# Weight casts and subtractions placed ahead of roots, reciprocals and the use of a finished unit, in a two-block model kernel on one Trainium2 core

## What is computed

```python
def rms_norm(x, g):
    xf = x.astype(jnp.float32)
    y = xf * lax.rsqrt(jnp.mean(xf * xf, axis=-1, keepdims=True) + RMS_EPS)
    return (y * g.astype(jnp.float32)).astype(x.dtype)
...
def conv_ffn(h, w_up, ffn_dw_w, ffn_dw_b, w_down):
    val, gate = jnp.split(h @ w_up, 2, axis=-1)
    gate = causal_dwconv(gate, ffn_dw_w, ffn_dw_b)
    return (jax.nn.silu(gate) * val) @ w_down
...
    h = x
    for l in range(DEPTH):
        u = rms_norm(h, norm_mix_g[l])
        h = h + mixer_sublayer(u, cos, sin, w_in[l], b_gate[l], ret_gn_g[l], w_ret_out[l],
                               conv_dw_w[l], conv_dw_b[l], conv_ln_g[l], conv_ln_b[l],
                               w_conv_out[l], b_conv_out[l], w_mix_out[l])
        mem_n = rms_norm(mem, norm_mem_g[l])
        h = h + memory_cross_attention(rms_norm(h, norm_xattn_g[l]), mem_n,
                                       w_xq[l], w_xkv[l], w_xo[l])
        h = h + conv_ffn(rms_norm(h, norm_ffn_g[l]), w_up[l], ffn_dw_w[l], ffn_dw_b[l], w_down[l])
    return rms_norm(h, norm_final_g)
```

## Time and profile before

| what | us |
|---|---|
| median of 3 runs | 2090.15 |
| lowest, highest | 2089.9, 2092.16 |
| the profiled execution, whole | 2091.13 |
| its span, first to last instruction | 2089.3 |
| TensorE busy in it | 2068.3 |
| VectorE busy | 1659.0 |
| ScalarE busy | 1055.8 |
| GpSimd busy | 257.6 |

### The profile page before, as it was taken

The page is one execution under the profiler, slowest core; times in us unless marked ns, Lnnn a source line. Parts: engine busy times, 40 slices in busy tenths (PEclk is TensorE's granted clock), DMA queues, the critical chain, the costliest instruction groups (busy, mean ns, idle before and its releaser), DMA issues.

```text
span 2089.3 us, 38625 instructions
## 1 busy us (share of the span) xinstructions
PE 2068.3 (99%) x16378; PEld 2015.3 (96%) x16378; DVE 1659.0 (79%) x2449; ACT 1055.8 (51%) x1282; POOL 257.6 (12%) x176
## 2 busy tenths in 40 slices
PE   9999999999999999999999999999999999999998
PEld 9999999999999999989999999999988999989998
DVE  8888797787779788798986768767698996758764
ACT  6786354356755434355545445444346445444442
POOL 0212055000006500001201001100000300000100
PEclk9999999999999999999999999999999999999999
DMA  6663455554235455544555435546544555534543
GB/s 262 193 199 125 182 185 184 170 212 150 101 142 182 157 187 202 181 158 162 199 178 174 177 141 182 176 159 212 182 164 150 192 182 182 182 139 167 182 163 118
DMA packets 58300, 361.95 MB, mean 173 GB/s; under 512 B 6736, under 2 KB 9360, under 8 KB 21136
## 3 DMA queue, kind: packets, MB, share of 16 engines
q1 hardware_dynamic: 58128, 359.48, 49.0%
HBM read 358.37 MB, written 1.08 MB: 172 GB/s over the span
## 4 chain that ended last, share of the span: by engine, by line
PE 95%; DVE 2%; ACT 1%; issue 1%; DMA 0%; POOL 0%; SPq 0%; DVEq 0%; ACTq 0%
PE acc L644 79%; PE acc L643 7%; PE acc L759 1%; PE acc L760 1%; PE acc L761 1%; PE acc L964 1%; PE pA L1013 1%; DVE w_lo L1196 0%; DMA raw<-in_wide 0%; PE pC L807 0%; PE pB L1037 0%; PE pD L1124 0%; PE pA L1099 0%; PE pB L1099 0%; PE pB L1124 0%
## 5 line engine op out<-in xcount | busy, mean ns | idle before, releaser
L644 PE MATMUL acc<-in_hi,w_hi 128*128 128x256 f32 x4656 | 1304.9, 285 | 9.8 <-issue 9.4
L644 PE MATMUL acc<-in_hi,w_lo 128*128 128x256 f32 x4656 | 1292.9, 283 | 0.1
L644 PE MATMUL acc<-in_lo,w_hi 128*128 128x256 f32 x4656 | 1230.2, 283 | 0.0
L644 PEld LDWEIGHTS acc<-in_hi,w_hi 128*128 128x128 f32 x4656 | 892.0, 192 | 16.2 <-issue 12.3
L644 PEld LDWEIGHTS acc<-in_hi,w_lo 128*128 128x128 f32 x4656 | 892.1, 192 | 0.6 <-DVE w_lo L1527 0.3
L644 PEld LDWEIGHTS acc<-in_lo,w_hi 128*128 128x128 f32 x4656 | 855.1, 192 | 1.2 <-issue 1.0
L1196 DVE TENSOR_TENSOR w_lo<-raw,w_hi 128x2048 fp32r<-128x2048 f32 (+1 forms) x341 | 737.3, 2164 | 112.7 <-ACT w_hi L2059 111.7
L2059 ACT CAST w_hi<-raw 128x2048 fp32r<-128x2048 f32 (+1 forms) x341 | 614.2, 1804 | 238.5 <-PE acc L644 227.6
L2659 POOL TENSOR_TENSOR in_lo<-arena,in_hi 128x256 fp32r<-128x256 f32 (+1 forms) x112 | 127.2, 1136 | 1212.4 <-ACT in_hi L2519 514.5
L1840 DVE SCALAR_TENSOR_TENSOR arena<-arena,cols 128x256 f32<-128x256 f32 x480 | 200.4, 487 | 0.0
L2669 POOL TENSOR_TENSOR arena<-arena 128x256 f32<-128x256 f32 x44 | 96.3, 2189 | 385.1 <-ACT arena L2341 385.1
(11 more groups left out here) (293 smaller groups left out, 1653.3 us busy)
## 6 DMA issues: line engine op xcount, KB each, us to landing
raw<-in_wide SPq DMA_DIRECT2D x285, 1024.0 KB, 4.8
raw<-in_narrow SPq DMA_DIRECT2D x64, 704.0 KB, 4.1
arena<-cs_rows SPq DMA_DIRECT2D x16, 256.0 KB, 5.0
arena<-in_mem SPq DMA_DIRECT2D x3, 1024.0 KB, 6.9
x<-in_x SPq DMA_DIRECT2D x4, 256.0 KB, 6.1
raw<-in_wide SPq DMA_DIRECT2D x2, 512.0 KB, 5.4
tables<-in_tables SPq DMA_DIRECT2D x1, 1024.0 KB, 17.1
arena<-cs_rows SPq DMA_DIRECT2D x16, 64.0 KB, 5.4
```

What stands on the lines that cost most here:

```text
L644: return mm(outs[m], w[:, k, at], moving[:, c, :], start=start, stop=stop)
```

## The change

Five things are changed. (1) The units in halves are gone; all units are cast and subtracted whole. TensorE's waits for half_hi and half_lo go with them (those hunks are left out below). (2) `early` is gone: VectorE subtracts unit u+2 ahead of `first` in all segments, up_b (from unit 8 on), ret_q and ret_k among them; in conv_out and the residuals the last unit (`last_first`) keeps the subtraction behind `first`, and in no other. (3) In front of a norm's root ScalarE casts unit 2, and behind it unit 3 ahead of the high parts; VectorE subtracts unit 2 ahead of the reciprocal and no longer amid the multiplies. The cross attention gets the same order. (4) At attention's end the cast and the subtraction of unit 90 go some steps ahead (they are left out of their place by `elsewhere`), and `att_norm(7, 1)` goes ahead of `att_high(6)`. (5) The steps of the angles in the second `down` go from units 1, 2 (VectorE) and 3 (ScalarE) to units 2, 4 and 5.

```diff
@@ -198,17 +198,7 @@
     base_of = lambda name: [s.base for s in segs if s.name == name]
-    stepped = {g: n + 2 for n, g in enumerate(sorted(
-        [base_of("ssm_out")[0] + 2, base_of("att_k")[0], base_of("att_o")[0] + 2, base_of("att_o")[0] + 3]
-        + base_of("glu") + [b + 2 for b in base_of("mix")]))}
-    split_behind = [b + 2 for b in base_of("mix")]
-
-    def halves_of_unit(g, buf):
-
-        if g == segs[2].base + 2:
-            return buf[:, 0:WIDE // 2], buf[:, WIDE // 2:]
-        both = buf[:].rearrange("p (k m n) -> p k m n", k=DC, m=2)
-        return both[:, :, 0, :], both[:, :, 1, :]
+    elsewhere = (base_of("att_o")[0] + 2,)
     col, ncol = column_names()
...
@@ -1185,13 +1166,6 @@
                 n = sizes[g]
-                if g in stepped:
-                    a, b, c = (halves_of_unit(g, v) for v in (w_lo[g % RAW], raw[g % RAW], w_hi[g % HI]))
-                    dve.wait_ge(half_hi, stepped[g])
-                    tt(a[0], b[0], c[0], ALU.subtract).then_inc(half_lo, 1)
-                    dve.wait_ge(hi_ready, g + 1)
-                    tt(a[1], b[1], c[1], ALU.subtract).then_inc(lo_ready, 1)
-                    return
                 dve.wait_ge(hi_ready, u + (seg.base + 1))
...
@@ -1201,7 +1175,7 @@
-            def project(name, first=None, second=None, steps=None, early=False, nth=None, behind=0):
+            def project(name, first=None, second=None, steps=None, last_first=False, nth=None, behind=0, at=6):
...
@@ -1211,9 +1185,9 @@
                     late = nth is not None and fixed and u < max(2, behind)
-                    ahead = (early or (fixed and u == seg.units - 1)) and (
-                        seg.base + j + 2 not in stepped or seg.base + j + 2 in split_behind)
-                    if not ahead and not late:
+                    ahead = last_first and fixed and u == seg.units - 1
+                    mine = not late and seg.base + j + 2 not in elsewhere
+                    if mine and not ahead:
                         split(u + 2, seg, j + 2)
...
@@ -1229,9 +1203,9 @@
                             split(u + 3, seg, j + 3)
-                        elif u == (7 if early else 6):
+                        elif u == at:
                             split(9, seg, 9)
-                    if ahead and not late:
+                    if mine and ahead:
                         split(u + 2, seg, j + 2)
...
@@ -1358,7 +1332,7 @@
                 marks = {"pair": 1 if twice or final else 0.5, "deep": 1, "feat": 2}[kind]
-                seg = project(name, first_and_last, second, steps={v_order: marks}, early=kind == "feat")
+                seg = project(name, first_and_last, second, steps={v_order: marks}, last_first=True)
                 E.passed(sum_ready, 1 + DC)
...
@@ -1393,10 +1367,9 @@
                 seg, half = take.next(), NORM_PIECES // 2
+                split(2, seg, 2)
                 reciprocal_std(rstd[:])
-                scaled(name, x, rstd, xn, val_ready, range(DC // 2))
-                split(2, seg, 2)
-                scaled(name, x, rstd, xn, val_ready, range(DC // 2, DC))
+                scaled(name, x, rstd, xn, val_ready)
                 scale_unit(seg, nth, 0)
...
@@ -1683,7 +1656,7 @@
                         tt(f_h[:, j % 2, :], f_s[:, j % 2, :], banks[0], ALU.mult).then_inc(acc_free, 1)
-                    project("up_b", first, second, steps={v_order: 2, silu_ready: 1}, early=True, nth=5 + 3 * l, behind=8)
+                    project("up_b", first, second, steps={v_order: 2, silu_ready: 1}, nth=5 + 3 * l, behind=8, at=7)
                     E.passed(inh_ready, FC)
...
@@ -1770,6 +1743,7 @@
                 att_recip(7, 1)
+                split(2, take.next(), 2)
                 att_low(6)
...
@@ -1789,14 +1763,14 @@
                     E.settle()
-                if j == 1:
+                if j == 2:
                     for part in TURN_PARTS:
...
                     E.settle()
-                if j == 2:
+                if j == 4:
                     E.mark(ts(k, r2, float(np.float32(np.pi)), -float(np.float32(2 * np.pi)), ALU.is_gt, ALU.mult))
...
@@ -1889,7 +1863,7 @@
                         qk_half[:] = o, take.base(), 8 * l + 2 * o
-                        project(n, rotary, lambda u, j, banks: conv_tap(l, u // 2 + o) if j % 2 == 0 else None, early=True)
+                        project(n, rotary, lambda u, j, banks: conv_tap(l, u // 2 + o) if j % 2 == 0 else None)
...
@@ -1958,7 +1932,7 @@
                         tt(y, y, gate[:, bass.ds(u * 2, 2), :], ALU.add).then_inc(val_ready, 1)
-                    project("conv_out", mixed, steps={v_order: 1}, early=True)
+                    project("conv_out", mixed, steps={v_order: 1}, last_first=True)
                     E.passed(inh_ready, 4)
...
@@ -1997,12 +1971,14 @@
                     q = take("mem_q")
+                    split(2, q, 2)
                     reciprocal_std(rstd[:])
...
                             x_max(l, u - 2)
-                        split(u + 2, q, u + 2)
+                        if u:
+                            split(u + 2, q, u + 2)
                         if u >= 2:
...
@@ -2051,11 +2027,6 @@
                     act.wait_ge(unit_done, u + (seg.base - HI + 1))
-                if g in stepped:
-                    a, b = (halves_of_unit(g, v) for v in (w_hi[g % HI], raw[g % RAW]))
-                    copy(a[0], b[0]).then_inc(half_hi, 1)
-                    copy(a[1], b[1]).then_inc(hi_ready, 1)
-                    return
                 copy(w_hi[g % HI][:, 0:n], raw[g % RAW][:, 0:n]).then_inc(hi_ready, 1)
...
@@ -2081,7 +2052,8 @@
                         return
-                    split(u + 2, seg, j + 2)
+                    if seg.base + j + 2 not in elsewhere:
+                        split(u + 2, seg, j + 2)
                     if use and not (isinstance(u, int) and u < lag):
...
@@ -2113,10 +2085,10 @@
                 seg = take.next()
+                split(2, seg, 2)
                 roots()
-                split(2, seg, 2)
+                split(3, seg, 3)
                 high_parts(xn, chunk0, NORM_PIECES, DC // NORM_PIECES, val_ready)
-                split(3, seg, 3)
...
@@ -2352,7 +2324,7 @@
                             norm_root()
-                        if layer == 1 and j == 3:
+                        if layer == 1 and j == 5:
                             act.wait_ge(ang_v, 1)
...
@@ -2449,8 +2422,8 @@
                 att_norm(7, 0)
+                att_norm(7, 1)
                 att_high(6)
-                att_norm(7, 1)
                 for part in range(3):
...
@@ -2602,9 +2575,12 @@
                     q = take("mem_q")
+                    split(2, q, 2)
                     norm_root()
+                    split(3, q, 3)
                     for u in range(4):
-                        split(u + 2, q, u + 2)
+                        if u >= 2:
+                            split(u + 2, q, u + 2)
                         if u >= 2:
```

More of the change, by code:

```diff
@@ L611, in body @@
                     g = seg.base + j
-                    if g in stepped:
-                        pe.wait_ge(half_hi, stepped[g])
-                        pe.wait_ge(half_lo, stepped[g])
-                    elif g:
+                    if g:
                         pe.wait_ge(hi_ready, u + (seg.base + 1))
@@ L670, in body @@
                         for m in range(tiles):
-                            if g in stepped and m == 1:
-                                pe.wait_ge(hi_ready, g + 1)
-                                pe.wait_ge(lo_ready, g + 1)
                             for k in range(nk):
@@ L709, in body @@
                                     pe.wait_ge(gin_ready, second_half)
-                                if g in stepped and m * nk + k == tiles * nk // 2:
-                                    pe.wait_ge(hi_ready, g + 1)
-                                    pe.wait_ge(lo_ready, g + 1)
                                 product(m, k, hi, in_hi, start=k == 0 and not (halves and j % 2))
```

1 line of the change is left out of this document (removed).

## The result

The changed kernel takes 2109.72 us (median of 4 runs, 2109.05 to 2111.06), the kernel before 2090.66 beside it (4 runs); the ratio is 1.0091, 95% interval 1.0074 to 1.0109. It is slower by 19.1 us, where 21.4 were forecast (2111.5, range 2104 to 2121).

The account below looks back on a forecast made before the run. TensorE, working through 99% of the span, was taken as the bound. A cost of 28.2 us in up_b less 7.0 us of gains elsewhere gave 21.2 us slower, median 2111.4 rounded up to 2111.5 us, range 2104 to 2121.

Parts of the forecast that it names:

- The ring: up_b: loop product, in_hi, cast, subtraction, taps, silu takes 7.03 us against TensorE's 5.76; costs 14.1 us a layer.
- the signs: Profile after: up_b subtractions 7.0 us apart from unit 10, some ten TensorE restarts a layer, earlier restarts smaller or gone.
- The wins: Outside up_b: TensorE waits removed at attention's end, norms, ret_q and ret_k, and second down; 7.0 us in all.
- At nothing: the halves of units 26, ...: Units 26, 70, 130, 188, 240, 298: dropping halves costs nothing, being done well before TensorE needs them; uncovered, 2 us a place.
- Attention's end: Attention's end into up_a: one subtraction less in VectorE's queue shrinks or removes restarts; gains 3.15 us.
- Its 1.24 for the x add: Attention's end: the x add that started at 602.92 comes 1.24 us earlier, shrinking the restart at 602.31.
- Its other 1.9: Behind the norm after attention: restarts of 0.90 and 0.6 go, and one of 0.4 at the first unit following.
- The norms: First layer's glu: subtraction ahead of the reciprocal fills a 1.68 us wait, last multiply 1.6 earlier; gains 1.4 us.
- ret_q and ret_k: First subtraction fits VectorE's 4.92 us wait before the first rotary; gains 0.8 us in each of two layers.
- The angles: Second down: spreading the angles' steps over later units removes the wait at 748.86; gains about 0.8 us.
- the rival with half clock in the ring's waits: up_b and down: clock falls in the waits; milder, up to 2121, 10 in 100; half throughout, 2200, 2 in 100.
- 201.22: Trace row before: TensorE's 1.70 us idle, then clock 0.50 for 3.4 us; taken to show such waits can halve the clock.

Follow-up runs that it names:

- the order alone: Kernel before with only up_b's subtraction put ahead of the taps from unit 8 on, in both layers: 2123.27 us, ratio 1.0158.

## Why the prediction was right, and where it was off

**The ring** held in all its parts. Its round was forecast as 7.03 us and measured as 7.02; the sum of start-to-start times from the trace before gave it, though no ring of this kind ran there. VectorE's subtractions stand 7.03 us apart from unit 10 on, as the signs said, and TensorE waits from unit 12 on, as the prediction's sums give; down's unit 2 was forecast at +14.1 in each layer and shifted by 14.3. The runs that undo the ring on VectorE's side and on ScalarE's side, the run with the order alone and the run that takes 0.5 us from the ring leave no other cause.

**The wins** were forecast as 7.0 us outside up_b and came to 10.3. The difference of 3.3 is mostly one step, "At nothing: the halves of units 26, ...": unit 26 gave 2.4 us. The prediction shows the wait there ([1.70 <-POOL in_lo]) and reads from it only what it does to the clock; it isn't in its list of what the change can win. I looked there for what TensorE loses without halves and not for what GpSimd gains when VectorE's operation starts later. Of the 2.4 us, 1.4 is the fallen clock of the profiled execution before, which the same wait doesn't bring in every profile, as the last section shows. 0.6 more came in the two downs (0.3 at unit 1 of each, 0.75 at unit 4 of the second, together 1.4 for 0.8), and 0.3 in xbc, which is no more than the scatter between kernels with the same code there. In the profiled executions the forecast was +21.2 us and the measured change +18.4: 3.3 from the wins, less 0.4 that up_b cost more. In the medians only 1.8 us are left of this (2109.7 for 2111.5), since the profiled execution before was 0.98 us above its median and that of the changed kernel was not. So the forecast is somewhat nearer than its terms are.

**Attention's end** was forecast at 3.15 and came at 3.1, in part by luck. Its 1.24 for the x add came as 1.3, made of 0.3 at the turning of the last head and 1.6 at the start of up_a 0, less 0.6 for the longer wait in the middle of up_a 0, which was not foreseen. Its other 1.9 came as 1.8; the run with the norms alone gives these 1.8, so they belong to the norm's order and not to attention's end. **The norms** were forecast at 1.4 in glu and came at 1.4. **ret_q and ret_k** were forecast at 0.8 a layer and came at 0.8 in both: 0.5 at the restart (forecast 0.59) and 0.3 in the units around it (forecast 0.2).

**The angles**: "the wait at 748.86 goes" was right, its cause wrong. The order outside up_b removes it with the angles unmoved, the last subtraction of up_a ahead of its taps being the likely part; the move of the angles does nothing. Right size, wrong step.

**The halves** at mix (units 188 and 298) were not free, as the prediction had it: without them each unit came 0.45 us later, and "well before TensorE ends the two units ahead" doesn't hold for these two. Unit 90, which its list leaves out, cost 1.2 us at its place. In the changed kernel none of this shows.

**The clock**: the rival with half clock in the ring's waits, 12 in 100 together, did not come. 2 x 10 waits of about 1.05 us idle and those around down (1.50, then 0.55 and 0.84) left it at 1.00. The prediction puts the first waits in down at about 1.8 us lost, that is under 1.6 idle, and calls 201.22 "no longer" than these; with its 1.70 idle it is the longer one, so that row didn't speak against the forecast.

## What to carry to other kernels

When the order of one engine's queue is changed, write down the ring: from an operation, through every wait on another engine's in-order queue, back to the same operation one unit later, and add the start-to-start times. It was 7.03 us here with both engines busy well under 5.76, so no sum of work shows it; a ring is broken as well by letting the other engine lag one unit. Of an operation that is moved ask too what it ran beside: two engines that exclude each other make a later start of one a gain for the other.

## What the runs showed of the hardware that was not expected

A wait of TensorE with 1.70 us idle ahead of its last low-part matmuls in ssm_out (1.69 in one profile) stands in the same code of five profiled kernels that keep unit 26 in halves. Behind it the granted clock was 0.50 in three of them (before, the order outside up_b alone, attention's end alone), and 1.00 in two (up_b's order alone and the norms alone). A stretch of 3.4 us behind it, for the norms alone:

```profile
202.00:205.40 3.40, 3.40 (x31) 1.00 0.71 243
```

and for attention's end alone, where the clock falls some 0.3 us into the stretch:

```profile
202.00:205.40 3.40, 3.40 (x19) 0.55 0.80 251
```

So the same wait sometimes costs 1.4 us more and sometimes not, which may be part of the spread of a kernel's runs (2088.7 to 2092.2 in 22 runs of before); a wait of 1.47 or 1.50 us idle never did in these traces, and one of 2.11 did once. What decides it between them these runs don't settle.

The Trainium skill, "TensorE: Matmul & The Clock Gate", HAM oscillation, warns of idle gaps of TensorE that are longer than any of these. By that rule none of these waits would cost the clock, and here the traces disagree: 0.50 behind 1.70 us idle.
